# A decoder step on one core: the last quad's output products by halves in six PSUM banks, and the waits for the final stores on SyncE in place of GpSimd

## The reference

```python
y = hres + hier_moe(rms_norm(hres, p['norm2']), ...)

def hier_moe(x, rg_w, rg_b, re_w, re_b, w1, w3, w2):
    # top-1 of 4 groups, top-2 of its 4 experts: gate is (tokens, 16), two entries not zero
    ...
    h = jax.nn.silu(jnp.einsum('nd,edf->nef', t, w1)) * jnp.einsum('nd,edf->nef', t, w3)
    h = h * gate[..., None].astype(h.dtype)
    return jnp.einsum('nef,efd->nd', h, w2).reshape(b, l, d)
```

## Time and profile before

| | |
|---|---|
| Median of three runs | 858.57 us (855.92, 858.57, 860.18) |
| The profiled execution | 858.98 us |
| Its span, first to last instruction | 857.2 us |
| TensorE busy | 800.2 us (93%) |
| VectorE busy | 382.9 us (45%) |
| ScalarE busy | 227.2 us (27%) |
| GpSimd busy | 279.3 us (33%) |
| Mean granted TensorE clock | 0.972 of full speed |

### The profile page before, as it was taken

How to read it: one execution, slowest core, us unless ns; L and a number is a source line. 1 busy time by engine, 2 the same in 40 slices (tenths; PEclk the granted TensorE clock), 3 DMA queues, 4 the chain that set the end, 5 groups by cost and what they waited for, 6 DMA issues and landing times. The chain is left out here.

```text
span 857.2 us, 14295 instructions
## 1 busy us (share of the span) xinstructions
PE 800.2 (93%) x5314; PEld 569.6 (66%) x5314; DVE 382.9 (45%) x700; ACT 227.2 (27%) x429; POOL 279.3 (33%) x204
## 2 busy tenths in 40 slices
PE   9999999989989898999999999999999789998990
PEld 8887777666658686777776777888888634333320
DVE  4671676757357678754551311533311622021110
ACT  4122333321413633313323222412201522011010
POOL 0000511354444773335443545522000022232223
PEclk9999999999989999999999999999999899999996
DMA  9233622245556431245553541251165679999952
GB/s 367 93 131 116 204 76 87 88 125 173 160 152 198 142 117 61 75 137 160 160 156 117 161 160 62 79 193 63 50 241 211 248 246 383 358 368 367 365 179 39
DMA packets 85450, 147.23 MB, mean 172 GB/s; under 512 B 13063, under 2 KB 46872, under 8 KB 85252
## 3 DMA queue, kind: packets, MB, share of 16 engines
q1 hardware_dynamic: 79012, 135.42, 46.9%
q0 software_dynamic: 5920, 10.82, 5.1%
q10 hardware_dynamic: 448, 0.06, 0.1%
HBM read 137.71 MB, written 18.90 MB: 183 GB/s over the span
## 5 line engine op out<-in xcount | busy, mean ns | idle before, releaser
L565 PE MATMUL ps<-xn,ring 128*128 128x268 f32 (+1 forms) x576 | 140.0, 399 | 1.0 <-ACT qb L1302 0.9
L565 PEld LDWEIGHTS ps<-xn,ring 128*128 128x128 f32 x576 | 109.3, 194 | 26.8 <-issue 3.7
L2394 POOL TENSOR_TENSOR kv<-kv,sgd 128x1024 f32<-128x1024 f32 (+1 forms) x32 | 79.1, 2489 | 121.4 <-DVE tmp L1742 70.2
L1445 ACT ACTIVATE sgt<-sgt,vec 128x260 f32<-128x260 f32 x60 | 30.1, 511 | 143.0 <-DVE sgt L2003 79.2
L810 PE MATMUL ps<-br,ring 128*128 128x260 f32 x256 | 63.2, 395 | 3.4 <-DVE sgt L2014 2.1
L2484 POOL DMA_INDIRECT out_y<-cst,gtab x24 | 37.3, 1556 | 80.5 <-DVE cst L2320 48.3
L841 PE MATMUL ps<-xn,ring 128*128 128x260 f32 x240 | 59.5, 391 | 1.3 <-ACT cst L1302 1.3
L841 PE MATMUL ps<-xn,qb 128*128 128x260 f32 x240 | 57.8, 384 | 1.6 <-DVE sgt L2004 1.6
L810 PEld LDWEIGHTS ps<-br,ring 128*128 128x128 f32 x256 | 48.3, 193 | 14.6 <-issue 2.8
L1048 PE MATMUL ps<-qk,ring 128*128 128x260 f32 x256 | 56.5, 383 | 0.0
L1048 PEld LDWEIGHTS ps<-qk,ring 128*128 128x128 f32 x256 | 48.6, 190 | 7.8 <-issue 0.4
(11 more groups left out here) (465 smaller groups left out, 1315.3 us busy)
## 6 DMA issues: line engine op xcount, KB each, us to landing
ring<-in_w_mg SPq DMA_DIRECT2D x32, 640.0 KB, 4.3
kv<-in_kc SPq DMA_DIRECT2D x128, 128.0 KB, 2.2
kv<-in_vc SPq DMA_DIRECT2D x128, 128.0 KB, 2.1
ring<-in_w_in SPq DMA_DIRECT2D x24, 512.0 KB, 4.5
kv<-in_w SPq DMA_DIRECT2D x8, 1024.0 KB
br<-in_w SPq DMA_DIRECT2D x8, 1024.0 KB, 17.0
sgd<-in_w SPq DMA_DIRECT2D x8, 1024.0 KB, 17.3
qk<-in_w SPq DMA_DIRECT2D x6, 1024.0 KB, 15.0
```

The costliest lines, as they stand in the source:

```text
L565: mm = pe.matmul(ps[:, 2 * (t % 2) + h, 0:hw], wsl(c, k), xnv[:, k, col0 + h * hw:col0 + (h + 1) * hw], start=(k == 0), stop=(k == KT - 1))
L1445: act.activation(g, g, ACT.Sigmoid, bias=vv(V_BM + 8 * "ABCD".index(n) + m + i)).then_inc(g_a, 1)
L2394: pool.tensor_tensor(kb, kb, qbc[:, b:b + 1, :].to_broadcast([P, HALF // 2 + (half and u), 256]), ALU.mult)\
```

## The change

In the last quad (tiles 9, 10, 11) TensorE calls `last_outputs()` in place of `outputs(q, 0)` to `outputs(q, 2)`. It makes half 0 of all three tiles, then half 1 of all three. Each of the six halves has a bank of its own: 3, 4, 5 for half 0 and 6, 7, 0 for half 1. The evictions read those banks and count `m_y` in the new order. And the waits for the last adds and for the stores move from the end of GpSimd's program to the end of SyncE's.

```diff
+LAST_OUT = [(3, 4, 5), (6, 7, 0)]
...
@@ sync
             sp.wait_ge(y_out, 16 * NB)
+            for stored, n in ((kv_out, 3), (rst_out, 1), (rs_out, 1), (outs, POOL_OUTS)):
+                sp.wait_ge(stored, 16 * n)
+            for r in range(ROUNDS):
+                sp.wait_ge(m_yst[r], 32 * QUADS)
...
@@ tensor
+            def last_outputs():
+
+                q = QUADS - 1
+                for n in range(2):
+                    for r in range(ROUNDS):
+                        if n == 0:
+                            pe.wait_ge(m_htev, ROUNDS * q + r + 1)
+                        elif r == 0:
+                            pe.wait_ge(m_ya, ROUNDS * q)
+                            pe.wait_ge(m_yd, ROUNDS * q)
+                        for f in range(2):
+                            w = weights(12 * q + KT + 2 * n + f)
+                            for g in range(4):
+                                rows = slice(32 * g, 32 * g + 32)
+                                mm = pe.matmul(ps[rows, LAST_OUT[n][r], :], hT[r][:, f, rows], w[:, g, :], start=(f == 0),
+                                               stop=(f == 1), tile_position=(0, 32 * g))
+                        mm.then_inc(m_y, 1)
...
+                if not more:
+                    last_outputs()
+                    break
                 outputs(q, 0)
...
@@ scalar
-                act.wait_ge(m_y, 2 * i + 1)
+                last = i >= TILES - ROUNDS
+                act.wait_ge(m_y, TILES - ROUNDS + i + 1 if last else 2 * i + 1)
...
-                act.activation(yb[i % ROUNDS][:, 0, :], ps[:, 6, :], ACT.Copy, scale=g_w[:, i:i + 1]).then_inc(m_ya, 1)
+                act.activation(yb[i % ROUNDS][:, 0, :], ps[:, LAST_OUT[0][i % ROUNDS] if last else 6, :], ACT.Copy, scale=g_w[:, i:i + 1]).then_inc(m_ya, 1)
...
@@ vector
-                dve.wait_ge(m_y, 2 * i + 2)
+                last = i >= TILES - ROUNDS
+                dve.wait_ge(m_y, TILES + i + 1 if last else 2 * i + 2)
...
-                ts(yb[i % ROUNDS][:, 1, :], ps[:, 7, :], g_w[:, i:i + 1], None, ALU.mult).then_inc(m_yd, 1)
+                ts(yb[i % ROUNDS][:, 1, :], ps[:, LAST_OUT[1][i % ROUNDS] if last else 7, :], g_w[:, i:i + 1], None, ALU.mult).then_inc(m_yd, 1)
...
@@ gpsimd
-            for r in range(ROUNDS):
-                pool.wait_ge(m_yst[r], 32 * QUADS)
-            for stored, n in ((kv_out, 3), (rst_out, 1), (rs_out, 1), (outs, POOL_OUTS)):
-                pool.wait_ge(stored, 16 * n)
```

More of the change, by code:

```diff
@@ L1230, in _ @@
                     rows_T(u + 3)
+                if not more:
+                    last_outputs()
+                    break
                 outputs(q, 0)
-                if more:
-                    rows_T(u + 4)
-                    rows_T(u + 5)
+                rows_T(u + 4)
+                rows_T(u + 5)
                 outputs(q, 1)
```

## The result

The change makes the kernel faster: 850.12 us (median of six runs, 848.40 to 851.36) against 857.25 (six runs of before, 854.65 to 860.18); ratio 0.9924, 95% interval 0.9897 to 0.9951. Between the medians that is 7.1 us, by the ratio 6.5 (4.2 to 8.8).

What follows compares the result with a forecast made beforehand. Bound: an unbranched closing string of TensorE, VectorE, GpSimd adds, landing and drain. Last add 1.37 us sooner and drain behind its end moved the end from 857.2 to 852.33: 858.57 - 4.9 = 853.7 us; 8-in-10 range 851.6 to 857.4.

Steps and rivals of the forecast that it cites:

- Part 1: Last quad's output products by halves: stall on sgd weights gone, last second-choice add 1.37 us sooner, at 846.67.
- 0.47 + 1.65 = 2.12 us lost: TensorE's stall on the two sgd weight blocks in tile 0's second half, all to be covered by reordering.
- are there: Last quad's first halves: the two br weight blocks they need were taken as already landed, so no wait.
- GpSimd's pitch: First-choice adds follow each other 1.855 us apart, behind evictions 1.72 apart; third add starts 1.87 us sooner.
- 1.37 with its slower landing: Gain at the last second-choice add if the third first-choice add lands after 4.7 us; 1.87 with 4.2.
- Part 1, the landings: Third first-choice add, now 1.855 us behind its neighbour, was taken to land after 4.7 us; lower bound 4.2.
- Rival (b): GpSimd's first two adds stand still during VectorE's overlapping evictions, costing 1.5 us: -3.4, 855.2 us; chance 0.05.
- the rule that the prediction set beside it: Trainium skill, SBUF: VectorE in a two-port mode locks GpSimd out, which then can't write descriptors.
- Part 2: Final waits moved to SyncE: GpSimd meets its drain at once, while adds are in flight; end at 852.33.
- I take it as 3.91 us behind the end of the last add: GpSimd's final drain as 3.91 us of work of its own, independent of landings: 846.67 + 1.55 + 3.91 = 852.13.
- Rival (a): GpSimd's drain starts its work only when the adds have landed: -1.4 us, 857.2 us; chance 0.17.
- SyncE's branch: SyncE's last waits after the landing at 851.37, then wake-up, waits and barrier: done at 852.03, 0.3 before the drain.

Runs made afterwards that it cites:

- e9: Kernel before with six banks for the last quad's outputs, order of products and final waits unchanged; ratio 1.0001 to the kernel before.
- e7: Products by halves, final waits on GpSimd, TensorE waiting for all four output blocks before the first product; ratio 1.0049 to the kernel before.
- e1: The kernel before once more, nothing edited; ratio 0.9994.
- e8: The kernel before, profiled again unedited; 14.3 us from first product to VectorE's last eviction, no whole-kernel time given.
- e12: The kernel before, profiled again unedited; 15.2 us from first product to VectorE's last eviction, no whole-kernel time given.
- e3: Kernel before with only the final waits moved from GpSimd to SyncE, products as before; ratio 0.9974 to the kernel before.
- e5: Kernel before plus one GpSimd drain behind the second-choice adds of quad 2; ratio 0.9968 to the kernel before.
- e10: Kernel before with only the last quad's products by halves, final waits left on GpSimd, run again; ratio 0.9938 to the kernel before.
- e11: Changed kernel plus one GpSimd drain behind the second-choice adds of quad 2; ratio 0.9895 to the kernel before.
- e4: The changed kernel once more, unedited; ratio 0.9887 to the kernel before.
- e2: Kernel before with only the last quad's products by halves, final waits left on GpSimd; 850.33 against 857.49 us, ratio 0.9924.
- e6: Changed kernel with its block closed without GpSimd's drain, waits still on SyncE; ratio 0.9915 to the kernel before.

## Why the prediction was wrong

**What bounds the kernel.** Right: the end is a string of TensorE, VectorE, GpSimd, landing and drain. Both parts shorten it.

**Part 1, the stall.** Here the prediction failed, in the step "0.47 + 1.65 = 2.12 us lost". The mechanism held: the order hides the loads of the `sgd` blocks (e9 has the banks and no gain, e7 has the order and the stall, and is slower). But the premise that the two `br` blocks "are there" did not hold in most executions: TensorE waited 0.5 to 1.1 us for the second one in five of the six by halves. The term was mis-sized, since it came from one execution that was not typical. From the first product to VectorE's last eviction, the profiles have, in us:

```
order of before:  12.7 (before)  13.6 (e1)  14.3 (e8)  15.2 (e12)  16.5 (e3)  16.8 (e9)  17.4 (e5)   mean 15.2
by halves:        10.6 (e10)  11.3 (e11)  11.5 (after)  11.7 (e4)  11.9 (e2)  11.9 (e6)             mean 11.5
```

The profile that I read is the smallest of seven. In it TensorE had lost time in quad 2, to waits and to a half-clock stretch at 792 us, where eight matmuls take 1.94 us and not 1.07:

```profile
789.70 1.07 PE L1206 MATMUL ps<-qb,cx 128*32 128x512 f32 x8 [1.40 <-DMA qb<-in_w]
792.31 1.94 PE L1206 MATMUL ps<-vtok,cx 128*32 128x512 f32 x8 [1.54 <-DMA vtok<-in_w]
```

So it came late to the last quad, when its weights were nearly there: the last block landed 4.7 us behind the first product. In the six others that is 5.6 to 7.3 us. Counted from one TensorE instruction at the end of quad 2's hidden products (784.4 us in before), TensorE reached the last quad's first product after 40.5 us in before, and after 35.6 to 38.9 in the six others; the last block landed after 45.2 us in before, and after 44.4 to 45.0 in five of the six (42.3 in e3). The weight stream went on while TensorE was held up there, so a delay ahead of this place shortens the stall in it. And in three of the seven (e3, e5, e9) the clock fell behind the stall, which it did in none of the six by halves. The mean difference is 3.7 us. GpSimd's pitch takes 0.26 of it, as forecast: its third add starts 1.60 us behind the eviction before, and 1.86 after. So 3.5 us stand where the prediction had 1.87 (1.37 with its slower landing).

**Part 1, the landings.** The third first-choice add, 1.85 us behind its neighbour, landed after 4.0 us in the change's profile and not after 4.7. Line 2511, the landings of the adds at 829.70 and 831.55, of which the least is the third add's:

```profile
DMA to landing us min/median/max: 4.0/4.6/5.2
```

In all fourteen profiles the third first-choice add landed after 3.8 to 4.2 us, 1.85 or 3.43 us behind its neighbour: adds close together with no weights flowing did not disturb each other. From the third first-choice add to the last second-choice add it was 8.4 to 8.8 us in either order, so the 3.5 arrive at the end. Rival (b) fell too: the add at 827.85 lay over VectorE's eviction at 827.97 and took 1.55 us. Every VectorE instruction that lay over an add here, the one at 796.06 in the earlier trace rows too, read from PSUM, and no trace shows which mode it was in. So these overlaps settle the rival for the evictions, but they do not test the rule that the prediction set beside it, and by that rule alone the rival need not hold.

**Part 2, the drain.** "I take it as 3.91 us behind the end of the last add" failed. The drain waits for the landings and ends 1.98 us behind the last one (after, e3, e4). From the last add to the end it is thus 6.5 to 6.9 us in place of 8.9 to 9.4, a gain of some 2.4 and not 3.5. Rival (a) had the wait for the landing right, but with the whole 3.91 behind it; half of that is done while the adds are in flight. What I took for fixed work grows with the DMAs that GpSimd issued since its last drain (e5, e11). SyncE's branch was sized well: it was done within 0.3 us of the landing. The sentence of the Trainium skill that the prediction weighed (PSUM — Partial Sum Buffer, Engine vs sequencer instructions: a drain waits until the engine is idle) is not all for GpSimd: in e5 the middle drain ended 7.8 us behind the engine's last instruction.

**The sum.** In the tail the means give 3.5 + 2.4 = 5.9 us, against 4.9 forecast: part 1 was taken 2.1 us too small and part 2 1.1 too large. That the two errors cancel in part is luck. Measured, by the ratios, are 6.5 us in the first runs (4.2 to 8.8) and 9.7 in e4 (7.2 to 12.2); for part 1 alone 6.5 (e2, 3.9 to 9.1) and 5.3 (e10, 2.8 to 7.7), against the 3.5 that the last quad shows. Of the 3.6 us between the forecast time of 853.7 and 850.12, 1.3 are not the change's at all: the forecast was taken off a median of 858.57 for the kernel before, which was 857.25 in the runs beside the result.

**What stays open.** Some 2 to 3 us of part 1. In the profiles TensorE reaches one instruction at the end of quad 2's hidden products at 782.6 us in the mean of the seven in the order of before, and at 780.9 in the mean of the seven by halves (e7 among them). From one execution to the next it differs by 2.8 and 2.0 (standard deviation), so that is no difference that can be told, and no instruction ahead of it is changed. The difference stands there already by 366 us (365.7 and 364.0 in the means, at one instruction of the mixer part), over 400 us ahead of the first product of the last quad, and is the same, 1.7 us, at both places. I have no mechanism by which part 1 could act there, and chance in 6 to 12 runs a kernel is not ruled out.

## What to carry to other kernels

The size of a stall on a DMA stream, read from one profile, is only as typical as the engine's arrival at it: compare when the block lands with when it is wanted, and look at several executions before its size goes into a sum. Where an engine waits for such a stream, put the products on the blocks that are already there first; spare banks make that possible and by themselves gave nothing here. Where GpSimd issues many DMAs, put a drain of it where it idles, or close the block without its drain when another engine has waited for the stores: behind the last landing that took some 1.7 us off here, too little to be told in the time of the whole kernel.

## What the runs showed of the hardware that I had not expected

GpSimd's drain took 3911 ns behind 47 DMAs that had all landed (before, e1, e2, e7 to e10, e12), and 543 ns behind six (e5). Begun ahead of the last landing, it ended 1.98 us behind it with 47 (after, e3, e4), 1.73 with 41 (the middle drains of e5 and e11) and 0.3 with six (e11). TensorE's granted clock fell to 1.2 GHz in a wait of 7.3 us (e7), and in three of seven executions behind waits of 0.5 to 1.7 us in a row (e3, e5, e9); in the four others it held at 2.4 GHz.
